# Half of a copy moved from ScalarE to VectorE, a store and a fill reordered on SyncE's queue, and an earlier bias add

## The chip, the cores and the metric

One core of a Trainium2 chip runs the whole kernel. The metric is the device time of one execution in microseconds; the time of a kernel is the median of its runs. TensorE (PE), VectorE (DVE), ScalarE (ACT), GpSimd (POOL) and SyncE (SP) each work through a program of their own in order, and wait for one another through semaphores. SyncE, ScalarE and GpSimd also issue the transfers (DMA).

## What is computed

One encoder layer on 512 tokens of 1024 features in fp32, then a final RMSNorm:

```
xn  = rmsnorm(h, g_mix)
proj = xn @ w_in + b_in                  # 1024 -> 2*512 (conv) + 3*512 (q, k, v)
conv = silu(layernorm(depthwise_conv31(a * sigmoid(g)) + conv_b))
attn = neighbourhood attention, 8 heads of 64, window 8 x 16, bias rpb[head, drow, dcol]
h   = h + [conv ; attn] @ w_out + b_out
h   = h + mixture of 32 experts, 4 of them for each token (clamped SwiGLU), on rmsnorm(h, g_ffn)
out = rmsnorm(h, g_final)
```

## The kernel before

Each fp32 product is made of three products: both operands are split into a high part (`..._high`, a cast made by ScalarE) and a low part (`..._low`, the difference, made by VectorE), and TensorE adds high x high, low x high and high x low.

**Start (to about 25 us).** The tokens are four tiles of 128. Per tile ScalarE squares and sums (L715), GpSimd makes rstd (L578, L580), VectorE makes xn (L1090), TensorE transposes it in two halves of four blocks into two PSUM banks (L1700), ScalarE copies each half to `xnT_high` (L703), and VectorE subtracts to get `xnT_low` (L1097). VectorE's program goes tile by tile: xn of tile n, then both low halves of tile n - 1. ScalarE's program puts the copies of tile 0 between the Squares of tile 2 and tile 3. Then VectorE copies the bias columns (L1102, L1103) and begins to split w_in (L1109).

**Projection (25 to about 141 us).** w_in comes in five loads of 2 MB (L467), issued by SyncE once x is loaded. TensorE makes 16 groups of 24 matmuls (L1714 to L1716; `proj_done` counts them), four for the gated input and its gate each, q and k, and then v by tiles. VectorE's program in the same time, written out by hand: the splits of w_in, the gated unit (L1117), 31 taps of the convolution for each of four channel blocks (L1130, L1134), and the bias tables of the eight heads (`tables`, L1154), two heads at a time, between splits and taps.

**Bias tables.** rpb is loaded to an SBUF tile (`rpb_tile`, 121 rows of 64 numbers) and stored 16 times to HBM (`rpb_pad`, L588, on GpSimd's queue). SyncE waits for all 16 stores (`rpb_stored`) and reads them back in another arrangement (`raw_bias`, L479), eight loads for each pair of heads. A pair's loads are issued only when the tables of the pair before are made, as they share a buffer.

**Zero fills.** The expert stage needs zeros in parts of `y_rows` in HBM. SyncE issues two fills from the SBUF tile `zeros` after the first pair's bias loads: the blocks past the thirtieth (`spare`, L482, counted by `y_stored`) and half-blocks of the others (L484). ScalarE waits for both before it copies v (L768, L769), as that overwrites `zeros`.

**b_out.** GpSimd adds it to h by four accumulating transfers (L593), once the eight tables are made. h is next used when w_out's products are added (L1197). After attention and w_out come the router and 32 experts with their weights streamed in; the change doesn't touch them.

Of the kernel before, what the change touches and what calls it, by code (L numbers as in the profile page):

```python
# [14 lines left out]
P = 128  # L15
SEQ, D_MODEL = 512, 1024
GRID_W, N_ROWS = 64, 8
QB = 16
NQ = GRID_W // QB
D_CONV, CONV_K = 512, 31  # L20
PAD = CONV_K // 2
HEADS, HEAD_DIM = 8, 64
# [13 lines left out]
CAP = 128  # L36
# [24 lines left out]
def encoder_kernel(nc, x, g_mix, w_in, b_in, conv_w, conv_b, ln_g, ln_b, rpb, w_out, b_out,  # L61
# [3 lines left out]
    with ctx:  # L65
        def sem(name):
            return ctx.enter_context(nc.semaphore(name))
# [70 lines left out]
        xnT_high = over("xnT_high", a_at, 0, [P, KD, SEQ])  # L138
# [35 lines left out]
        zeros = area_t[:, 2112:2112 + HALF]  # L174
# [126 lines left out]
        rstd_ready = sem("rstd_ready")  # L301
        xn_ready = sem("xn_ready")
        xn_transposed = sem("xn_transposed")
        xnT_first = sem("xnT_first")
        xnT_act = sem("xnT_act")
        xnT_low_ready = sem("xnT_low_ready")
        win_high_ready = sem("win_high_ready")
# [148 lines left out]
        @block.sync  # L456
        def _(sp):
            for n in range(NQ):
                sp.dma_start(h[:, n, :], x_blocks[n]).then_inc(x_loaded[n], 16)
            sp.dma_start(stage[0:20, 0, :], b_in[0].rearrange("(c p) -> c p", p=P)).then_inc(stage_loaded, 16)  # L460
            sp.dma_start(stage[0:CONV_K * CC, 1, :],
                         conv_w[0].rearrange("k (c p) -> (k c) p", p=P)).then_inc(stage_loaded, 16)

            for n in range(NQ):
                sp.wait_ge(x_loaded[n], 16)
            for i, col in enumerate((1, 0, 2, 3, 4)):
                sp.dma_start(unit(1 + i), win_v[:, :, col * HALF:(col + 1) * HALF]).then_inc(win_loaded[i], 16)  # L467

            spare = y_rows[LATE * CAP:, :].rearrange("(p i) (j f) -> p (i j) f", p=CAP, f=HALF)
            sp.wait_ge(rpb_stored, 16 * QB)  # L470
            copy_size = (HEADS * RPB_H + 1) * RPB_PITCH
            for pair in range(HEADS // 2):
                if pair:
                    sp.wait_ge(tables_ready, 8 * pair)
                for r in range(N_ROWS):
                    start = (2 * pair * RPB_H + WIN_H - 1 - r) * RPB_PITCH + QB - 1
                    src = bass.AP(rpb_pad.tensor, rpb_pad.offset + start,
                                  [[copy_size - 1, QB], [RPB_H * RPB_PITCH, 2], [1, RUN]])
                    sp.dma_start(raw_bias[r::N_ROWS, :, :], src).then_inc(raw_loaded, 16)  # L479
                if pair == 0:  # L480
                    sp.wait_ge(zeros_ready, 1)
                    sp.dma_start(spare, zeros[0:CAP].unsqueeze(1).to_broadcast([CAP, spare.shape[1], spare.shape[2]])).then_inc(y_stored, 16)  # L482
                    halves = y_rows[0:LATE * CAP, :].rearrange("(m s i) (j f) -> (i j) m s f", s=4, i=SMALL, f=HALF)[:, :, 2, :]
                    sp.dma_start(halves, zeros.unsqueeze(1).to_broadcast([P, LATE // 2, HALF])).then_inc(halves_zeroed, 16)  # L484
            def load(i, e):
                sp.dma_start(w_raw[i][:, :], piece_src(i, e)).then_inc(raw_piece[i], 16)

            sp.wait_ge(proj_done, 12)
            sp.dma_start(unit(1), wout_v[:, :, HALF:]).then_inc(wout_loaded[1], 16)
            sp.wait_ge(proj_done, 20)  # L490
            sp.dma_start(unit(6), wout_v[:, :, 0:HALF]).then_inc(wout_loaded[0], 16)
            for i in range(3):
                load(i, 0)
            sp.wait_ge(wout_done, 2 * NQ)
            for i in range(3, 5):
                load(i, 0)
            sp.wait_ge(xn2_stored, 16 * NQ)
            sp.wait_ge(xn2_transposed, 2 * NQ)
            sp.wait_ge(xg_loaded, 16)
            for i in (5, 6, 7, 8, 9, 11):  # L500
                load(i, 0)

            def reload(i, e, at):
                sp.wait_ge(piece_used, at + 1)
                load(i, e)

            def expert_at(b):
                return sp.value_load(order[0:1, bass.ds(b, 1)], min_val=0, max_val=N_EXPERTS - 1)

            sp.wait_ge(order_ready, 1)  # L510
            second = expert_at(1)
            for i in range(GATE, DOWN):
                if i == UP:
                    sp.wait_ge(overflow_ready, 2)
                    sp.wait_ge(gate_rows_ready, 1)
                    load(10, 0)
                reload(i, second, i)
            with sp.Fori(0, N_EXPERTS - 2) as j:
                e = expert_at(j + 2)
                for i in range(DOWN):  # L520
                    reload(i, e, PIECES * j + 8 + i)
                e = expert_at(j + 1)
                for i in range(DOWN, PIECES):
                    reload(i, e, PIECES * j + 8 + i)
            final = expert_at(N_EXPERTS - 1)
            for c in range(4):
                sp.wait_ge(piece_used, PIECES * (N_EXPERTS - 2) + 8 + UP + c + 1)
                sp.dma_start(w_raw[UP + c][:, :], piece_src(DOWN + c, final)).then_inc(raw_piece[UP + c], 16)
            trips = sp.value_load(n_ovf[0:1, 0:1], min_val=0, max_val=MAX_OVERFLOW)
            with sp.If(trips > 0):  # L530
                sp.wait_ge(late_added, NQ)
                with sp.Fori(0, trips) as t:
                    e = sp.value_load(ovf_exp[0:1, bass.ds(t, 1)], min_val=0, max_val=N_EXPERTS - 1)
                    for i in range(PIECES):
                        reload(i, e, EXTRA_BASE - PIECES + PIECES * t + i)
            for n in range(NQ):
                sp.wait_ge(final_ready, n + 1)
                sp.dma_start(out_blocks[n], out_tile[n]).then_inc(out_stored, 16)
            sp.wait_ge(out_stored, 16 * NQ)
# [3 lines left out]
        def _(pool):  # L543
# [39 lines left out]
                pool.wait_ge(ss_ready, n + 1)  # L583
                rstd_of(n, ss_ready)

            pool.wait_ge(rpb_tile_loaded, 16)
            for c in range(QB):
                pool.dma_start(rpb_pad[c], rpb_tile[:, :]).then_inc(rpb_stored, 16)  # L588

            pool.wait_ge(xn_ready, NQ)  # L590
            pool.wait_ge(tables_ready, 4 * HEADS)
            for n in range(NQ):
                pool.dma_start(h[:, n, :], row_bcast(b_out, D_MODEL), accum_op=ALU.add).then_inc(bout_added, 16)  # L593

# [97 lines left out]
        def _(act):  # L692
# [5 lines left out]
                              vec[0].rearrange("(c p) -> c p", p=P)).then_inc(stage_loaded, 16)  # L698
            def xnT_half(n):

                for half, high_done in enumerate((xnT_first, xnT_act)):
                    act.wait_ge(xn_transposed, 2 * n + half + 1)
                    s.copy(xnT_high[:, 4 * half:4 * half + 4, n * P:(n + 1) * P],  # L703
                           bank[4 + (2 * n + half) % 4][:, :].rearrange("p (k t) -> p k t", k=4)).then_inc(high_done, 1)

            def pT_out(i):

# [3 lines left out]
            for n in range(NQ):  # L711
                act.wait_ge(x_loaded[n], 16)
                if n:
                    act.wait_ge(ss_ready, n)
                s.activation(junk_norm[n % 2], h[:, n, :], ACT.Square, accum_out=ss[:, n:n + 1]).then_inc(ss_ready, 1)  # L715
                if n == NQ - 2:
                    xnT_half(0)
            for n in range(1, NQ):
                xnT_half(n)
            def win_high_part(g):  # L720
                loaded, high, _ = split_parts(g)
# [61 lines left out]

            act.wait_ge(glu_ready, 16)
            act.wait_ge(tables_ready, 1)
            act.wait_ge(y_stored, 16)
            act.wait_ge(halves_zeroed, 16)
            for n in range(NQ - 1):
                v_out(n)
# [265 lines left out]
        def _(dve):  # L1055
# [29 lines left out]
            for n in range(NQ + 1):  # L1085
                if n < NQ:
                    dve.wait_ge(rstd_ready, n + 1)
                    if n >= 2:
                        dve.wait_ge(xn_transposed, 2 * (n - 1))
                    v.scalar_tensor_tensor(xn_tile[:, n % 2, :], h[:, n, :], rstd[:, n:n + 1], gmix_row,  # L1090
                                           ALU.mult, ALU.mult).then_inc(xn_ready, 1)
                if n:
                    tokens = slice((n - 1) * P, n * P)
                    for half, high_done in enumerate((xnT_first, xnT_act)):
                        dve.wait_ge(high_done, n)
                        ks = slice(4 * half, 4 * half + 4)
                        v.tensor_tensor(xnT_low[:, ks, tokens],  # L1097
                                        bank[4 + (2 * (n - 1) + half) % 4][:, :].rearrange("p (k t) -> p k t", k=4),
                                        xnT_high[:, ks, tokens].bitcast(F32), ALU.subtract).then_inc(xnT_low_ready, 1)
# [45 lines left out]
            def tables(hd):  # L1145
                if hd == 0:
                    dve.wait_ge(mask_step, 15)
                    dve.wait_ge(proj_done, 8)
                dve.wait_ge(raw_loaded, 16 * N_ROWS * (hd // 2 + 1))

# [983 lines left out]
```

## Time and profile before

| | |
|---|---|
| median of 3 runs | 1336.9 us (1336.35 to 1338.11) |
| profiled execution | 1338.11 us, of it the span of the profile 1336.3 us |
| TensorE busy | 1269.6 us (95%) |
| VectorE busy | 1227.8 us (92%) |
| ScalarE, GpSimd busy | 972.3 us (73%), 182.7 us (14%) |
| moved by DMA | 473.31 MB, mean 354 GB/s |

The profile comes from one execution; times inside it are microseconds from the start of the span. SPq and ACTq are the queues of SyncE and ScalarE; the duration of an issue in them is how long the issuing program was held by it, and its landing is when the data was there. In a timeline the bracket behind a row gives the idle time before it and what ended it.

### The profile page before, as it was taken

The numbers are of one execution on the slowest core, as the hardware profiler recorded it, in microseconds if no ns is written. First come the engines' busy times: TensorE is split into PE (matmuls) and PEld (weight loads), VectorE is DVE, ScalarE is ACT, GpSimd is POOL, SyncE is SP. The second block draws the span as 40 slices with busy tenths as digits, with TensorE's granted clock in tenths as the row PEclk, the third lists the DMA queues.
The fourth block names the chain that finished last, engine by engine and source line by source line (L and its number), as shares of the span: only waits on it lengthen the run. The fifth ranks groups of instructions, "written<-read, shape, count | busy, mean of one in ns | idle before, by whom it ended". The sixth has DMA issues, their size and how long they took to land.

```text
span 1336.3 us, 17611 instructions
## 1 busy us (share of the span) xinstructions
PE 1269.6 (95%) x5771; PEld 1011.6 (76%) x5771; DVE 1227.8 (92%) x1010; ACT 972.3 (73%) x788; POOL 182.7 (14%) x181
## 2 busy tenths in 40 slices
PE   4999889789999999999999999999999999999996
PEld 4887668667878778787777777878777777777775
DVE  6799956699999999999999999999999999999997
ACT  4241664448797978788888888797979787878762
POOL 5001000112010101010110102020101010101252
PEclk9999889889999999999999999999999999999999
DMA  9945401499999999999999999999999999999984
GB/s 284 389 170 142 157 1 52 150 365 400 397 401 422 409 421 409 419 410 421 409 420 409 417 410 422 408 418 414 409 419 411 422 409 418 407 419 421 408 319 157
DMA packets 83974, 473.31 MB, mean 354 GB/s; under 512 B 10059, under 2 KB 10358, under 8 KB 34790
## 3 DMA queue, kind: packets, MB, share of 16 engines
q1 hardware_dynamic: 71726, 436.57, 81.1%
q0 software_dynamic: 7072, 19.39, 4.6%
q10 hardware_dynamic: 5144, 16.93, 3.4%
q8 instruction: 18, 0.29, 0.1%
q14 instruction: 14, 0.11, 0.0%
HBM read 447.72 MB, written 29.33 MB: 357 GB/s over the span
## 4 chain that ended last, share of the span: by engine, by line
PE 69%; DVE 15%; DMA 6%; ACT 5%; issue 3%; ACTq 1%; SPq 0%; POOL 0%; DVEq 0%
PE pair L1936 14%; PE pair L1937 13%; PE pair L1938 13%; PE pair L1952 6%; PE pair L1953 6%; DMA w_raw<-in_w_up 6%; DVE w_low L1283 5%; DVE area_m L1134 4%; ACT w_high L833 2%; PE pair L1923 2%; PE pair L1971 2%; PE pair L1950 1%; PE pair L1714 1%; PE pair L1715 1%; PE pair L1716 1%
## 5 line engine op out<-in xcount | busy, mean ns | idle before, releaser
L1283 DVE TENSOR_TENSOR w_low<-w_raw,w_high 128x2048 fp32r<-128x2048 f32 x380 | 838.2, 2245 | 41.3 <-ACT w_high L833 40.0
L833 ACT CAST w_high<-w_raw 128x2048 fp32r<-128x2048 f32 x380 | 703.0, 1878 | 170.5 <-PE pair L1938 117.5
L1936 PE MATMUL pair<-w_high,xT_high 128*128 128x512 f32 x528 | 211.2, 400 | 0.0
L1937 PE MATMUL pair<-w_low,xT_high 128*128 128x512 f32 x528 | 206.6, 391 | 0.0
L1938 PE MATMUL pair<-w_high,xT_low 128*128 128x512 f32 x528 | 206.0, 390 | 0.0
L1952 PE MATMUL pair<-w_high,xS 128*128 128x512 f32 x450 | 183.3, 407 | 0.1
L1953 PE MATMUL pair<-w_low,xS 128*128 128x512 f32 x450 | 175.7, 390 | 0.0
L1936 PEld LDWEIGHTS pair<-w_high,xT_high 128*128 128x128 f32 x528 | 99.1, 188 | 31.9 <-issue 11.4
L1938 PEld LDWEIGHTS pair<-w_high,xT_low 128*128 128x128 f32 x528 | 99.2, 188 | 21.6
L1937 PEld LDWEIGHTS pair<-w_low,xT_high 128*128 128x128 f32 x528 | 99.2, 188 | 19.2
L1936 PE MATMUL pair<-w_high,hT_high 128*128 128x512 f32 x256 | 102.1, 399 | 11.1 <-DVE w_low L1283 11.1
L1952 PEld LDWEIGHTS pair<-w_high,xS 128*128 128x128 f32 x450 | 84.5, 188 | 21.8 <-issue 3.6
L1937 PE MATMUL pair<-w_low,hT_high 128*128 128x512 f32 x256 | 100.5, 393 | 0.0
L1938 PE MATMUL pair<-w_high,hT_low 128*128 128x512 f32 x256 | 100.3, 392 | 0.0
L1953 PEld LDWEIGHTS pair<-w_low,xS 128*128 128x128 f32 x450 | 84.6, 188 | 20.4 <-issue 3.6
L1952 PE MATMUL pair<-w_high,hS 128*128 128x512 f32 x240 | 95.0, 396 | 0.0
L1953 PE MATMUL pair<-w_low,hS 128*128 128x512 f32 x240 | 93.5, 389 | 0.0
L1134 DVE SCALAR_TENSOR_TENSOR area_m<-area_u,convT,area_m 128x512 f32<-128x512 f32 x120 | 84.0, 755 | 0.4
L615 POOL CAST sel_in<-is_expert 128x128 fp32r (+1 forms) x17 | 42.6, 2504 | 272.0 <-PE pair L1953 246.9
L1936 PEld LDWEIGHTS pair<-w_high,hT_high 128*128 128x128 f32 x256 | 48.4, 189 | 23.7 <-DVE w_low L1283 12.2
L618 POOL CAST shift_sel<-is_expert 64x64 fp32r x15 | 14.1, 938 | 362.3 <-PE pair L1938 354.1
L1938 PEld LDWEIGHTS pair<-w_high,hT_low 128*128 128x128 f32 x256 | 48.5, 189 | 10.4
(355 smaller groups left out, 1800.5 us busy)
## 6 DMA issues: line engine op xcount, KB each, us to landing
w_raw<-in_w_gate SPq DMA_DIRECT2D x128, 1024.0 KB, 15.5
w_raw<-in_w_up SPq DMA_DIRECT2D x128, 1024.0 KB, 16.9
w_raw<-in_w_down SPq DMA_DIRECT2D x128, 1024.0 KB, 16.8
ring<-in_w_in SPq DMA_DIRECT2D x5, 2048.0 KB, 18.7
y_rows<-area_t SPq DMA_DIRECT2D x1, 8704.0 KB
y_rows<-area_m ACTq DMA_DIRECT2D x15, 512.0 KB
ring<-in_w_out SPq DMA_DIRECT2D x2, 2048.0 KB, 7.9
y_rows<-area_t SPq DMA_DIRECT2D x1, 3840.0 KB, 38.6
```

The costliest lines, as they stand in the source:

```text
L615: g.tensor_copy(sel_in[:, :], is_expert[:, bass.ds(e, 1)].to_broadcast([P, CAP])).then_inc(sel_in_ready, 1)
L618: g.tensor_copy(shift_sel[SMALL:, SMALL:], is_expert[SMALL:, bass.ds(e, 1)].to_broadcast([SMALL, SMALL])).then_inc(sel_in_ready, 1)
L833: s.copy(w_high[:, i % HIGH_RING, raw:], w_raw[i][:, raw:]).then_inc(high_ready, 1)
L1134: v.scalar_tensor_tensor(mixedT[:, c, :], u_pad[:, c, k:k + SEQ], convT[:, k * CC + c:k * CC + c + 1], mixedT[:, c, :], ALU.mult, ALU.add) ...
L1283: v.tensor_tensor(w_low[i][:, raw:], w_raw[i][:, raw:], w_high[:, i % HIGH_RING, raw:].bitcast(F32), ALU.subtract).then_inc(low_ready, 1)
L1923: last = t.transpose(bank[6 + k // 4][:, (k % 4) * CAP:(k % 4 + 1) * CAP], h_tok[:, k::KD], ident[0:CAP, 0:CAP])
L1936: t.matmul(to[half], tok_high, hi, start=(opens and kk == 0), stop=False)
L1937: t.matmul(to[half], tok_high, lo, start=False, stop=False)
L1938: last = t.matmul(to[half], tok_low, hi, start=False, stop=(k == KD - 1))
L1952: t.matmul(to[half], rows, w_high[:, i % HIGH_RING, cols], start=(opens and kk == 0), stop=False)
L1953: last = t.matmul(to[half], rows, w_low[i][:, cols], start=False, stop=(k == KD - 1))
L1971: t.matmul(to[half], sel[:, :], rows[:, half * HALF:(half + 1) * HALF], start=True, stop=False)
```

## The change

Four edits, all ahead of the expert stage:

1. ScalarE copies only the second half of each transposed tile, and does so after all four Squares. VectorE copies the first half itself, right ahead of the two subtractions.
2. The `spare` fill is issued by SyncE right behind the loads of w_in. The 16 stores of rpb_pad move from GpSimd's queue to SyncE's, behind this fill. The half-block fill stays behind the first pair's bias loads.
3. The wait for the `spare` fill moves from ScalarE (ahead of the v copies) to VectorE (ahead of the first bias table).
4. GpSimd issues the b_out transfers after twelve projection groups, and not after the tables.

```diff
@@ SyncE
             spare = y_rows[LATE * CAP:, :].rearrange("(p i) (j f) -> p (i j) f", p=CAP, f=HALF)
+            sp.wait_ge(zeros_ready, 1)
+            sp.dma_start(spare, zeros[0:CAP].unsqueeze(1).to_broadcast([CAP, spare.shape[1], spare.shape[2]])).then_inc(y_stored, 16)
+            sp.wait_ge(rpb_tile_loaded, 16)
+            for c in range(QB):
+                sp.dma_start(rpb_pad[c], rpb_tile[:, :]).then_inc(rpb_stored, 16)
             sp.wait_ge(rpb_stored, 16 * QB)
...
                 if pair == 0:
-                    sp.wait_ge(zeros_ready, 1)
-                    sp.dma_start(spare, zeros[0:CAP].unsqueeze(1).to_broadcast([CAP, spare.shape[1], spare.shape[2]])).then_inc(y_stored, 16)
@@ GpSimd
-            pool.wait_ge(rpb_tile_loaded, 16)
-            for c in range(QB):
-                pool.dma_start(rpb_pad[c], rpb_tile[:, :]).then_inc(rpb_stored, 16)
-
             pool.wait_ge(xn_ready, NQ)
-            pool.wait_ge(tables_ready, 4 * HEADS)
+            pool.wait_ge(proj_done, 12)
@@ ScalarE
-                for half, high_done in enumerate((xnT_first, xnT_act)):
-                    act.wait_ge(xn_transposed, 2 * n + half + 1)
-                    s.copy(xnT_high[:, 4 * half:4 * half + 4, n * P:(n + 1) * P],
-                           bank[4 + (2 * n + half) % 4][:, :].rearrange("p (k t) -> p k t", k=4)).then_inc(high_done, 1)
+                act.wait_ge(xn_transposed, 2 * n + 2)
+                s.copy(xnT_high[:, 4:8, n * P:(n + 1) * P],
+                       bank[4 + (2 * n + 1) % 4][:, :].rearrange("p (k t) -> p k t", k=4)).then_inc(xnT_act, 1)
...
-                if n == NQ - 2:
-                    xnT_half(0)
-            for n in range(1, NQ):
+            for n in range(NQ):
                 xnT_half(n)
...
-            act.wait_ge(y_stored, 16)
@@ VectorE
                 if n:
+                    dve.wait_ge(xn_transposed, 2 * (n - 1) + 1)
                     tokens = slice((n - 1) * P, n * P)
-                    for half, high_done in enumerate((xnT_first, xnT_act)):
+                    v.tensor_copy(xnT_high[:, 0:4, tokens],
+                                  bank[4 + 2 * (n - 1) % 4][:, :].rearrange("p (k t) -> p k t", k=4)).then_inc(xnT_dve, 1)
+                    for half, high_done in enumerate((xnT_dve, xnT_act)):
                         dve.wait_ge(high_done, n)
...
             def tables(hd):
                 if hd == 0:
                     dve.wait_ge(mask_step, 15)
+                    dve.wait_ge(y_stored, 16)
                     dve.wait_ge(proj_done, 8)
```

## Rows read from the trace of the kernel before

**Rows 1.** The page, part 4: shares of the chain that ended last.
```profile
PE 69%; DVE 15%; DMA 6%; ACT 5%; issue 3%; ACTq 1%; SPq 0%; POOL 0%; DVEq 0%
```

**Rows 2.** The chain of waits, 0 to 330 us: start, us, what.
```profile
24.86 0.77 PE pair L1714
...
71.56 1.23 DVE area_u L1117 x4
```

**Rows 3.** Busy time by stretch.
```profile
core 0: us, PE busy (x) PEld busy (x) DVE busy (x) ACT busy (x) POOL busy (x), PEclk, DMA share, GB/s
...
44.00:47.00 3.00, 3.00 (x15) 2.49 (x14) 2.86 (x5) 1.63 (x2) 0.00 (x0) 1.00 1.08 274
...
50.00:70.00 20.00, 20.00 (x89) 16.54 (x89) 19.39 (x32) 3.24 (x4) 0.00 (x0) 1.00 1.05 408
...
78.00:80.00 2.00, 2.00 (x11) 1.65 (x10) 2.00 (x4) 1.58 (x2) 0.00 (x0) 1.00 0.15 57
```

**Rows 4.** Timeline of ScalarE, 0 to 62 us.
```profile
14.67 1.06 ACT L715 ACTIVATE area_t<-h 128x1024 f32<-128x1024 f32 x1
...
28.68 2.94 ACT L730 CAST glu_high<-ring 128x1024 fp32r<-128x1024 f32 x3 [5.32 <-DMA ring<-in_w_in]
```

**Rows 5.** Timeline of VectorE, 0 to 62 us.
```profile
15.41 1.27 DVE L1090 SCALAR_TENSOR_TENSOR area_q<-h,rstd,area_k 128x1024 f32<-128x1024 f32 x1
```

**Rows 6.** Timeline of SyncE's queue, from several stretches up to 106 us.
```profile
14.41 16.26 SPq L467 DMA_DIRECT2D ring<-in_w_in  x5
...
25.48 5.18 SPq L467 DMA_DIRECT2D ring<-in_w_in  x1
...
30.71 5.55 SPq L479 DMA_DIRECT2D area_m<-rpb_pad  x1
...
40.73 0.59 SPq L479 DMA_DIRECT2D area_m<-rpb_pad  x1
...
42.03 20.55 SPq L484 DMA_DIRECT2D y_rows<-area_t  x1
78.95 26.72 SPq L479 DMA_DIRECT2D area_m<-rpb_pad  x24
...
100.69 1.80 SPq L479 DMA_DIRECT2D area_m<-rpb_pad  x3
```

**Rows 7.** Groups of VectorE's instructions by form, 0 to 300 us.
```profile
L1270 DVE COPY area_q<-pair 128x512 f32<-128x512 f32 x2 | 1.4, 685 | 0.0
```

**Rows 8.** Timeline of GpSimd, 0 to 62 and 90 to 260 us.
```profile
17.32 8.47 POOL L588 DMA_DIRECT2D rpb_pad<-area_t  x16
...
111.90 3.64 POOL L593 DMA_DIRECT2D h<-in_b_out  x4 [86.11 <-DVE ring L1154]
```

**Rows 9.** Timeline of VectorE, 60 to 165 us.
```profile
75.51 0.68 DVE L1154 SCALAR_TENSOR_TENSOR area_t<-area_m 128x192 f32<-128x192 f32 x2
...
86.39 0.68 DVE L1154 SCALAR_TENSOR_TENSOR area_t<-area_m 128x192 f32<-128x192 f32 x2
...
107.93 0.68 DVE L1154 SCALAR_TENSOR_TENSOR area_t<-area_m 128x192 f32<-128x192 f32 x2
```

**Rows 10.** DMA issues, 0 to 300 us; last column median to landing.
```profile
y_rows<-area_t SPq DMA_DIRECT2D x1, 3840.0 KB, 38.6
area_m<-rpb_pad SPq DMA_DIRECT2D x32, 64.0 KB, 2.3
h<-in_b_out POOLq DMA_DIRECT2D x4, 512.0 KB, 8.6
...
rpb_pad<-area_t POOLq DMA_DIRECT2D x16, 30.2 KB, 4.8
```

**Rows 11.** DMA issues, 41 to 42 us, the bias load issued last.
```profile
area_m<-rpb_pad SPq DMA_DIRECT2D x1, 64.0 KB, 8.6
```

**Rows 12.** DMA issues, 26 to 31 us, the w_in load issued last.
```profile
ring<-in_w_in SPq DMA_DIRECT2D x1, 2048.0 KB, 22.5
```

**Rows 13.** Timeline of ScalarE, 92 to 96 us.
```profile
93.32 0.69 ACT L748 ACTIVATE area_q<-pair,small 128x512 f32<-128x512 f32 x1 [3.81 <-PE pair L1716]
```

**Rows 14.** Busy time by stretch, columns as in the third group.
```profile
152.00:172.00 20.00, 17.28 (x90) 13.32 (x88) 16.62 (x41) 11.83 (x35) 0.00 (x0) 0.66 0.15 59
192.00:196.00 4.00, 3.93 (x22) 3.68 (x21) 1.63 (x9) 2.18 (x9) 0.00 (x0) 0.65 0.00 0
```

More of the change, by code:

```diff
@@ L303, in encoder_kernel @@
         xn_transposed = sem("xn_transposed")
-        xnT_first = sem("xnT_first")
+        xnT_dve = sem("xnT_dve")
         xnT_act = sem("xnT_act")
```

## The prediction

> **What bounds the kernel now.** I read the page first: of the chain that ended last PE has 69% and VectorE 15% [rows 1]. The diff touches only what runs before the expert loop, so the chain of waits of the first 330 us came next, and it shows who sets the pace there [rows 2]. TensorE begins the projection with w_in at 24.86, and the chain stays on its matmuls until 71.56. There it goes over to VectorE, and it stays on VectorE's program (splits of w_in, bias tables, convolution taps) without an idle gap to about 135. Attention and the router follow on the same chain. So every microsecond by which 24.86 moves, or by which VectorE stalls between 71 and 135, should arrive at the end. Nothing in that stretch waits for a fixed time: the weights of the expert loop are fetched on counts of finished projections.
>
> Then the timelines (VectorE and ScalarE at the start, SyncE's queue, VectorE at the tables) and the table of stretches. Transfers are the hidden resource: between 50 and 70 the DMA engines are full at 408 GB/s [rows 3], and what flows there is the zero fill of y_rows, which nobody needs before 120. The reader should see how near the small transfers lie to their use: each group of eight bias loads comes in just ahead of the table that reads it.
>
> **Part 1, half of the xnT_high copies goes from ScalarE to VectorE.** Before, ScalarE puts the two copies of tile 0 ahead of the Square of tile 3 (which starts at 14.67 [rows 4]), and VectorE goes to xn of tile 2 at 15.41 [rows 5]. After, ScalarE squares all four tiles first. The Square of tile 3 cannot start before its x is there, about 14.4 (SyncE waits for the same load and sends w_in at 14.41 [rows 6]); with the 1.1 us of a Square (1.06 busy) the one copy left for tile 0 runs at 15.5 and ends at 16.05 (0.58 busy). VectorE, which works in order, waits for it ahead of xn of tile 2, and subtracts for 0.6: xn of tile 2 starts at 16.7 and not 15.41.
>
> From there VectorE has two xn (1.27 busy, of which the next operation overlaps some 0.08: 1.2 each), and for each of the tiles 1, 2 and 3 one copy and two subtractions, nine operations. The same kind of copy stands in the router stage, 0.69 us busy like a subtraction [rows 7], 0.6 when the next follows at once. So 16.7 + 2.4 + 9 x 0.6 = 24.5 where before it was 23.0 (after them come 0.5 us of column copies and the first split of w_in, 1.2, and then the matmul of 24.86). The idle time inside the old sequence is already used up in this. ScalarE's part ends about 24.4, in time for the split. Four hand-overs inside VectorE may add up to 0.3. I take 1.6 us; ends 1.3 (no hand-over costs anything, x comes a little earlier) and 2.2 (a tenth more for each of the six operations that follow a hand-over). The cover: none. TensorE waits for exactly this split before 24.86, and its second group's weights come for either start in time (ScalarE starts on them at 28.68 [rows 4], and the first group's 24 matmuls last until 33.3), so the whole 1.6 reaches 71.56. Nothing else is late.
>
> **Part 2, the order on SyncE's queue.** Before, GpSimd issues the 16 stores of rpb_pad at 17.32 (8.47 us [rows 8]) and SyncE, when the five w_in issues end (14.41 + 16.26 = 30.7), sends eight bias loads, then the big fill, then the half-block fill [rows 6]. After, the order on SyncE is w_in, big fill (8704 KB), 16 stores, wait for all of them, eight loads, half-block fill (3840 KB). What is late is the first table, at 75.51 [rows 9]. Step by step:
> - From 44 to 47 the rate falls to 274 GB/s, from about 390 to 408 on either side: that is the passage of the eight small loads, so w_in's bytes are through at 44 and the fills begin at 47; 12.85 MB at 0.408 MB/us are 31.5 us, which ends at 78.5 as the table of stretches shows [rows 3]. After, w_in is rid of the stores' 0.5 MB (1.2 us), so the big fill runs from 42.8 for 21.8 us to 64.6.
> - An issue behind the fill doesn't return at once: the half-block fill's issue took 20.55 us, until 62.58, 15.6 us after the big fill began to flow [rows 6]. The first store's issue should return 15.6 after 42.8, at 58.4. Fifteen more at 0.6 (issues of this queue when nothing blocks it: three in 1.80 from 100.69, so the eighth starts some 4.4 after the first [rows 6]) end at 67.4; landing takes 2.3 (bias loads) to 4.8 (the old stores beside w_in) [rows 10]: 69.7 to 72.2.
> - Eight loads, 4.4 + 2.3 = 6.7: the first pair of tables has its data at 76.5 to 79. One engine or two trickle at 57 GB/s for 2.3 us behind a fill [rows 3], a reason against the low end. I take 77.6.
> - VectorE wants the table at 75.51 + 1.6 = 77.1. Parts 1 and 2 don't add, the later of the two counts: 77.6 - 75.51 = 2.1 us. The new wait for the big fill, ahead of the same table, ends long before (about 67), and behind it stand all of VectorE's splits and taps, for which TensorE waits in turn.
>
> **Part 2, second pair.** Its loads are asked for when the first tables are made (3.44 us after the first starts) and are needed 7.44 us after that (78.95 to 86.39 [rows 6, 9]), and take 6.8: they have 0.65 to spare. The half-block fill used to be nearly over by then (issued at 42.03, landed 38.6 later [rows 6, 10]). After, it is issued at 69.8 + 4.95 = 74.8, flows from 76 for 9.6 us and has its tail to 87.9. The loads sit behind it. Before, the last of the eight behind w_in landed 1.3 us after it (40.73 + 8.6 = 49.3 [rows 6, 11] against 25.48 + 22.5 = 48.0 [rows 12]); so 89.2, with the need at 77.6 + 3.44 + 7.44 = 88.5. I take 0.7, ends 0 and 3.
>
> **Part 3, b_out at twelve projections.** It starts at 93.32 + the delay (when ScalarE takes up the twelfth) instead of 111.90 [rows 8, 13]. Its four issues take 3.6 us and each transfer 8.6 [rows 10], together some 13, so they run while the third and fourth pair of loads come in; those have 0.7 and 0.5 us to spare (the latter: last issue at 105.1, landed 107.4, table at 107.93 [rows 9]). A load that shares engines should need up to twice its 2.3; but most of b_out is over at 106. I take 0.5, ends 0 and 2.5. Its old place cost nothing and it saves nothing: h is next touched past 200.
>
> **A rule that speaks against part 2.** The rows: stores on GpSimd's queue landed in 4.8 us although w_in filled the engines, while a bias load, on SyncE's own queue behind w_in, took 8.6 where alone it takes 2.3 [rows 10, 11]. The Trainium skill (DMA: Bandwidth & Descriptors, Queues, rings and completion order) says that an engine takes turns between queue rows by packet, but takes one ring's descriptors in order. By that rule the stores lose their turns and stand behind the whole fill, as I reckoned from the rows; without it they would be in HBM near 51 (the issue next after w_in returned at 36.3 [rows 6], sixteen at 0.6, and 4.8 to land) and part 2 would cost nothing; that is the first rival below. The old landing times agree with the rule; no row of before shows a small store behind a fill.
>
> The ScalarE wait for the big fill that goes cost nothing: it was reached after 120. Sum: 2.1 + 0.7 + 0.5 = 3.3 us. On the profiled execution (1338.1, span 1336.3) that gives 1341.4; it lay 1.2 above the median of the runs, so **1340.2 us**.
>
> **Rivals.**
> - Only the start counts (1.6 us or less): the fill lets the stores pass, or drains sooner, and the tables find their data. For it: 76.5 is a possible arrival, and I place the stall by differences of half a microsecond between long transfers. Against it: the 20.55 us issue. Time 1336.9 + 1.6 = 1338.5, with the start at its low end 1338.2.
> - The queue costs more: 121 rows of 256 bytes to a store may drain slowly, tables reached at 80 (4.5), the second pair 3, b_out 2.5: 10 us, 1346.9.
> - Faster, by the clock. At 152 to 172 the granted clock is 0.66 with TensorE busy 17.28 of the 20 us, and 0.65 at 192 to 196 with 3.93 [rows 14]. Full clock would save 0.34 x 17.28 + 0.35 x 3.93 = 7.3 us at most. If the shift leaves TensorE without these low stretches, 1336.9 + 3.3 - 7.3 = 1332.9. The sign turns once more than 3.3 of the 7.3 is saved, the 0.2% once more than 6. Against it: everything moves together, so the sparse pattern ahead of the drop comes again; and much of this busy time is beside other work. The same could go the other way.
> - The change does nothing (everything is covered): no; VectorE had no cover for its copies.
>
> **How the numbers follow.** 0.2% is 2.7 us, about what a measurement of this kernel can tell from no change. Forecast (2.7 to 7 us more) 0.50, costly queue 0.09, start only 0.33, faster clock 0.08 (of which 0.02 stays within the bound). Slower 0.59, same 0.34, faster 0.07. The forecast's own range is 1339.6 to 1344. The range for 8 in 10 takes in the start-only case with some gain of clock, 1336.5, and most of the costly queue, 1345.
>
> **What the new profile would show.** First matmul of the projection near 26.4, xn of tile 2 at 16.7. On SyncE's queue the first store's issue as a long one, until about 58, the last store near 67. A gap of VectorE ahead of the first table, ended by a DMA, first table at 77 to 79. A smaller gap ahead of the third table. b_out near 96. From 135 on the same steps as before, 3 us later. The prediction is wrong if the first store's issue returns at once, if VectorE goes without a gap from 73 to 135, if the ring behaves otherwise with small rows, or if TensorE's clock falls at other places.

## The result

The change makes the kernel slower: 1346.64 us against 1338.11 us for the kernel before, timed beside it (medians of seven runs each), a ratio of 1.0057 with a 95% interval of 1.0040 to 1.0075, so 7.6 us (5.4 to 10.0); the two medians alone lie 8.5 us apart. I had forecast 3.3 us more. The direction was right, the size was not. The median of the kernel before is 1.2 us higher here than the one that the prediction started from, so the difference, and not the absolute time, is what to compare. The granted clock adds scatter: three of the seven runs, at a mean granted clock of 0.977, took 1348.5 to 1349.3 us, the four at 0.980 to 0.983 took 1343.4 to 1346.6.

### The profile after

This is one execution of 1343.44 us with a span of 1341.7 us (the seven runs lie between 1343.4 and 1349.3; it is one of the shorter ones). The page's head and its chain (answer to [rows 1]):

```profile
span 1341.7 us, 17612 instructions
...
PE 67%; DVE 14%; DMA 7%; ACT 6%; issue 3%; SPq 1%; ACTq 1%; POOL 0%; DVEq 0%
```

TensorE and VectorE have lost shares to DMA, ScalarE and SyncE's queue. The timeline of VectorE at the start (answers to [rows 5]):

```profile
15.72 0.69 DVE L1098 TENSOR_TENSOR xnT_low<-pair,xnT_high 128x512 fp32r<-128x512 f32 x1 [0.71 <-ACT xnT_high L704]
16.33 1.28 DVE L1088 SCALAR_TENSOR_TENSOR area_q<-h,rstd,area_k 128x1024 f32<-128x1024 f32 x1
```

VectorE waits 0.71 us for ScalarE's one copy of tile 0 and starts xn of tile 2 at 16.33. TensorE's timeline (answers to [rows 2]):

```profile
26.34 0.76 PE L1716 MATMUL pair<-xnT_high,glu_high 128*128 128x512 f32 x1 [3.59 <-DVE win_low L1110]
```

The first matmul starts at 26.34 where it was 24.86. But x came 0.44 us earlier in this execution (ScalarE's first Square starts at 7.58, before at 8.02), so by these two traces the edit itself cost 1.9. SyncE's queue (answers to [rows 6]; the last row is the first store's issue by itself):

```profile
14.13 15.22 SPq L467 DMA_DIRECT2D ring<-in_w_in  x5
29.39 5.30 SPq L471 DMA_DIRECT2D y_rows<-area_t  x1
34.73 33.26 SPq L477 DMA_DIRECT2D rpb_pad<-area_t  x16
69.11 5.03 SPq L487 DMA_DIRECT2D area_m<-rpb_pad  x8
74.18 0.59 SPq L490 DMA_DIRECT2D y_rows<-area_t  x1
79.55 33.33 SPq L487 DMA_DIRECT2D area_m<-rpb_pad  x24
...
34.73 22.77 SPq L477 DMA_DIRECT2D rpb_pad<-area_t  x1
```

The first store's issue alone is held for 22.77 us, until 57.5. The 16 are issued by 68.0, and the first bias load goes at 69.11. The tables on VectorE (answers to [rows 9]):

```profile
76.14 0.67 DVE L1156 SCALAR_TENSOR_TENSOR area_t<-area_m 128x192 f32<-128x192 f32 x2
...
89.02 0.69 DVE L1156 SCALAR_TENSOR_TENSOR area_t<-area_m 128x192 f32<-128x192 f32 x2 [1.93 <-DMA area_m<-rpb_pad]
...
104.59 0.68 DVE L1156 SCALAR_TENSOR_TENSOR area_t<-area_m 128x192 f32<-128x192 f32 x2 [4.61 <-DMA area_m<-rpb_pad]
...
115.14 0.66 DVE L1156 SCALAR_TENSOR_TENSOR area_t<-area_m 128x192 f32<-128x192 f32 x2
```

The four pairs of tables start 0.6, 2.6, 7.3 and 7.2 us later than before. So there is no gap ahead of the first pair, 1.93 us ahead of the second, and 4.61 us ahead of the third. The chain of waits shows what the second and the third waited for (start, us, what):

```profile
80.12 1.37 SPq L487
...
86.58 2.42 DMA area_m<-rpb_pad
...
96.94 7.62 DMA area_m<-rpb_pad
```

The second pair's loads stood behind the half-block fill. The second to the fourth were slow to be issued, 1.37 us each instead of 0.6, and the first, issued at 79.55, landed 7.4 us later at 86.98, just behind the fill itself (issued at 74.18, landed at 86.69). Two short stretches of the DMA issues have both:

```profile
y_rows<-area_t SPq DMA_DIRECT2D x1, 3840.0 KB, 12.5
...
area_m<-rpb_pad SPq DMA_DIRECT2D x1, 64.0 KB, 7.4
```

The last load of the third pair was issued in time and then took 7.62 us to land instead of 2.3. What ran beside it stands in GpSimd's timeline (answers to [rows 8, 10]):

```profile
94.52 3.69 POOL L595 DMA_DIRECT2D h<-in_b_out  x4 [78.40 <-PE pair L1718]
```

and in the list of DMA issues:

```profile
h<-in_b_out POOLq DMA_DIRECT2D x4, 512.0 KB, 10.9
```

b_out's four transfers start 2 us after the third pair's first load; the median of their landings is 10.9 us after the issue.

### The profile page after: what moved, and what is told of

It is laid out like the page before. It is cut to its first block, busy times and chain, and to the rows that moved or that the text cites. A ratio compares the mean times of both kernels' runs of the same rounds, so it can differ in the third digit from the quotient of the medians.

```text
span 1341.7 us, 17612 instructions
## 1 busy us (share of the span) xinstructions
PE 1270.3 (95%) x5771; PEld 1012.1 (75%) x5771; DVE 1230.4 (92%) x1014; ACT 969.7 (72%) x784; POOL 174.0 (13%) x165
## 4 chain that ended last, share of the span: by engine, by line
PE 67%; DVE 14%; DMA 7%; ACT 6%; issue 3%; SPq 1%; ACTq 1%; POOL 0%; DVEq 0%
PE pair L1938 14%; PE pair L1939 13%; PE pair L1940 13%; DMA w_raw<-in_w_up 6%; PE pair L1954 5%; PE pair L1955 5%; DVE w_low L1285 5%; ACT w_high L831 3%; DVE area_m L1135 3%; PE pair L1925 2%; PE pair L1973 2%; PE pair L1952 1%; PE pair L1716 1%; PE pair L1717 1%; PE pair L1718 1%
## 5 line engine op out<-in xcount | busy, mean ns | idle before, releaser
L1938 PE MATMUL pair<-w_high,hT_high 128*128 128x512 f32 x256 | 102.0, 399 | 10.9 <-DVE w_low L1285 10.9
L620 POOL CAST shift_sel<-is_expert 64x64 fp32r x15 | 14.6, 971 | 363.1 <-PE pair L1940 363.1
## 6 DMA issues: line engine op xcount, KB each, us to landing
w_raw<-in_w_up SPq DMA_DIRECT2D x128, 1024.0 KB, 16.7
```

The source lines that it names most:

```text
L620: g.tensor_copy(shift_sel[SMALL:, SMALL:], is_expert[SMALL:, bass.ds(e, 1)].to_broadcast([SMALL, SMALL])).then_inc(sel_in_ready, 1)
L1938: t.matmul(to[half], tok_high, hi, start=(opens and kk == 0), stop=False)
```

## The experiments

Each kernel was timed with the kernel before beside it in five rounds. The medians of before were 1336.7, 1337.7 and 1336.6 us in the three sets. "gaps" are idle times of VectorE ended by a bias load, ahead of the four pairs of tables.

### First set: the parts alone

**b_out early, all else as before.**

```diff
-            pool.wait_ge(tables_ready, 4 * HEADS)
+            pool.wait_ge(proj_done, 12)
```

> The kernel before with the b_out edit alone (wait for twelve projections). Theory A (overlap): b_out costs what its packets take from the bias loads in flight beside them, one packet of 0.29 us ahead of each of theirs. Here the third pair's loads start at 89.8 and are all but home when b_out's data flows at 95, and the fourth pair's (100.7 to 105.6) meet its second half. Gap ahead of the third table 0 to 1 us, ahead of the fourth 0.5 to 2, time 1 to 3 us longer. Theory B (fixed price): b_out costs the 4.6 us of the changed kernel wherever it starts among the pairs; 4.5 to 5 us longer.

Ratio 1.0033 (1.0020 to 1.0046), 4.4 us longer. VectorE's timeline:

```profile
99.13 0.68 DVE L1154 SCALAR_TENSOR_TENSOR area_t<-area_m 128x192 f32<-128x192 f32 x2 [3.41 <-DMA area_m<-rpb_pad]
```

The whole price sits ahead of the third pair, nothing ahead of the fourth. By time it is nearer to theory B, though the gap, 3.41 us, is smaller than B's 4.6. Theory A had the place wrong: I thought the third pair's loads would be all but home. Seven were. The DMA issues of two short stretches, with the seventh load (issued at 91.93) and then the eighth (issued at 92.56):

```profile
area_m<-rpb_pad SPq DMA_DIRECT2D x1, 64.0 KB, 2.9
...
area_m<-rpb_pad SPq DMA_DIRECT2D x1, 64.0 KB, 6.5
```

The eighth took 6.5 us and landed at 99.10, where the table was waiting. One load of 64 KB, met by b_out's first data, holds VectorE for 3.4 us. The packets of the DMA engines show how. Between 94.6 and 96.4, with the eighth load under way, they are (packets, MB, share of 16 engines; q0 is GpSimd's queue; SyncE's, q1, has no line, as it has no packet here):

```profile
q0 software_dynamic: 83, 0.34, 101.8%
```

For 1.8 us not one packet of the bias load started.

**The change with b_out put back.**

```diff
-            pool.wait_ge(proj_done, 12)
+            pool.wait_ge(tables_ready, 4 * HEADS)
```

> The changed kernel with b_out back behind all tables. Theory A and B: the 4.6 us gap ahead of the third table goes, the 1.9 us gap ahead of the second stays; taps end 2.6 us later than before, time 2.6 us longer than before. Rival (the rest of the difference lies elsewhere, for instance in TensorE's granted clock in the attention stage): still 5 us or more longer.

Ratio 1.0043 (1.0029 to 1.0057), 5.7 us longer. The 4.61 us gap is gone, the one ahead of the second pair is 1.51. The tables come some 3 us late with the start, the measured time says 5.7; it was run again (third set).

**The copies alone** (ScalarE's and VectorE's part of the change, and no other).

> The kernel before with the copy edit alone. Theory (as the two traces show it): the first projection matmul starts 1.5 us later but fewer of its matmuls run at the slow rate, so that VectorE's gated unit starts only 0.6 us later; time 0.6 us longer, not told from none. My prediction's step: the whole 1.6 us arrives.

Ratio 1.0012 (1.0004 to 1.0021), 1.6 us longer, with no gaps. The prediction's step held and not the reading of two traces: how many of the first group's 24 matmuls take 0.43 us instead of 0.227 differs from execution to execution, 14 in the trace of before, 10 in that of after, 6 to 13 in the experiments (none in the one made to remove them), at either start. The first tables of the two traces lie only 0.6 us apart because of this chance and of the earlier x.

**The order on SyncE's queue alone** (fill and stores ahead of the bias loads on SyncE, wait for the fill on VectorE).

```diff
+            sp.wait_ge(zeros_ready, 1)
+            sp.dma_start(spare, ...).then_inc(y_stored, 16)
+            sp.wait_ge(rpb_tile_loaded, 16)
+            for c in range(QB):
+                sp.dma_start(rpb_pad[c], rpb_tile[:, :]).then_inc(rpb_stored, 16)
             sp.wait_ge(rpb_stored, 16 * QB)
...
                     dve.wait_ge(mask_step, 15)
+                    dve.wait_ge(y_stored, 16)
```

> The kernel before with the fill and stores on SyncE's queue in the new order, with its wait, alone. Theory: no gap ahead of the first table or 0.3 us (the first pair lands about 76), a gap of 2 to 2.6 us ahead of the second pair's, no gap ahead of the third and fourth; time 2 to 2.6 us longer. Rival (prediction's split): most of the cost sits ahead of the first table.

Ratio 1.0024 (1.0013 to 1.0035), 3.2 us longer. VectorE's timeline:

```profile
75.57 0.68 DVE L1153 SCALAR_TENSOR_TENSOR area_t<-area_m 128x192 f32<-128x192 f32 x2 [1.26 <-DMA area_m<-rpb_pad]
...
88.97 0.68 DVE L1153 SCALAR_TENSOR_TENSOR area_t<-area_m 128x192 f32<-128x192 f32 x2 [2.42 <-DMA area_m<-rpb_pad]
```

With the earlier start VectorE asks for the first pair at 74.3 and its data comes at 75.5. So the first pair's data is late too, and in the full change the copy edit hides that, as I had said: the later of the two counts, not their sum.

### Second set: what in each part costs

**b_out written and not added** (this leaves x out of the residual; the experts' loads become uneven, so that its total time of 1509.57 us can't be compared, and only the first 110 us are read).

```diff
-                pool.dma_start(h[:, n, :], row_bcast(b_out, D_MODEL), accum_op=ALU.add).then_inc(bout_added, 16)
+                pool.dma_start(h[:, n, :], row_bcast(b_out, D_MODEL)).then_inc(bout_added, 16)
```

> As the b_out edit alone, but the four transfers write b_out over h and don't add it (this leaves out x in the residual). Theory A (it is the adding: each engine has a 3.7 KB add packet of 0.29 us in turn with every packet of the bias loads, and there is 2 MB to read as well as to write): plain packets are about half as long, b_out is gone in half the time, the gap ahead of the third table falls from 3.4 to 0 to 1.5 us and the time to 0 to 2 us above before. Theory C (any transfer on another queue takes the same turns): the gap stays near 3.4 and the time near 4.4 above.

b_out lands in 6.4 us instead of 9.7, but the gap grows:

```profile
100.34 0.68 DVE L1154 SCALAR_TENSOR_TENSOR area_t<-area_m 128x192 f32<-128x192 f32 x2 [4.55 <-DMA area_m<-rpb_pad]
```

The last two loads took 6.6 and 6.7 us, no less than beside the adding transfers. The adding is not what costs; theory A is out. Of the larger gap 1.1 us is that the eighth load was issued later (93.66, in the edit alone 92.56). Here too no packet of SyncE's queue started for 1.8 us (94.4 to 96.2):

```profile
q0 software_dynamic: 171, 0.63, 102.2%
```

**Only the big fill first, the stores on GpSimd's queue as before.**

```diff
+            sp.wait_ge(zeros_ready, 1)
+            sp.dma_start(spare, ...).then_inc(y_stored, 16)
             sp.wait_ge(rpb_stored, 16 * QB)
...
-                    sp.dma_start(spare, ...).then_inc(y_stored, 16)
```

> The kernel before with only the big fill moved ahead of the first bias loads on SyncE's queue; the stores stay on GpSimd's. Theory (the stores behind the fill are what delays the first and so the second pair): the first pair's loads sit behind the fill and land near 68, ahead of the need at 74 to 75.5, the half-block fill goes as before; no gaps, time within 1 us of before. Rival (the fill's order itself does it): gaps as in the order edit, 3 us longer.

Ratio 0.9998 (0.9989 to 1.0007), and no gaps. SyncE's queue:

```profile
30.44 6.09 SPq L471 DMA_DIRECT2D y_rows<-area_t  x1
36.58 29.88 SPq L481 DMA_DIRECT2D area_m<-rpb_pad  x8
66.50 1.60 SPq L484 DMA_DIRECT2D y_rows<-area_t  x1
77.48 26.79 SPq L481 DMA_DIRECT2D area_m<-rpb_pad  x24
```

The first pair's loads wait behind the fill, but it is one passage. With the stores on this queue there are two, one after the other, since the loads read what the stores wrote: the stores are issued until 68.0 in the full change, and the loads only then.

**The order edit with the half-block fill behind the last pair's loads.**

```diff
                     sp.dma_start(raw_bias[r::N_ROWS, :, :], src).then_inc(raw_loaded, 16)
-                if pair == 0:
-                    halves = ...
-                    sp.dma_start(halves, ...).then_inc(halves_zeroed, 16)
+            halves = ...
+            sp.dma_start(halves, ...).then_inc(halves_zeroed, 16)
```

> The order edit alone, with the half-block fill moved behind the fourth pair's loads. Theory: the gap ahead of the second pair's table (2.4 us in the order edit alone) goes, the 1.3 us gap ahead of the first stays; time 1 to 1.5 us above before instead of 3.2. Rival (the second pair is late because the first is late): the gap stays, time 3 us above.

Ratio 1.0016 (1.0006 to 1.0026), 2.1 us longer where the order edit alone cost 3.2. VectorE's timeline:

```profile
76.29 0.67 DVE L1152 SCALAR_TENSOR_TENSOR area_t<-area_m 128x192 f32<-128x192 f32 x2 [0.87 <-DMA area_m<-rpb_pad]
87.19 0.67 DVE L1152 SCALAR_TENSOR_TENSOR area_t<-area_m 128x192 f32<-128x192 f32 x2
```

The gap ahead of the second pair is gone, the one ahead of the first stays. So the second gap is the half-block fill. The times by themselves would not tell the two kernels apart (0.8 to 3.5 and 1.7 to 4.7 us), the gaps do.

**TensorE kept busy ahead of its first group.**

```diff
+            for _ in range(12):
+                t.transpose(bank[1][:, 0:P], ident[:, :], ident[:, :])
             pe.wait_ge(xnT_low_ready, 2 * NQ)
```

> The kernel before with twelve transposes of the identity into an unused bank, run by TensorE while it waits for the first split of w_in. In the runs so far 7 to 14 of the first group's 24 matmuls went at the slow rate (0.43 against 0.227 us). Theory (the idle 3 to 4 us ahead of the first matmul are why it starts slow): 0 to 5 slow ones, VectorE's gated unit 1 to 2.5 us earlier, time 1 to 2 us below before. Rival: slow matmuls stay 7 to 14 whatever precedes them, time the same.

No slow matmul is left (TensorE's timeline):

```profile
21.51 2.73 PE L1710 MATMUL pair<-ident 128*128 128x128 f32 x12
25.07 0.47 PE L1716 MATMUL pair<-xnT_high,glu_high 128*128 128x512 f32 x1 [0.83 <-DVE win_low L1109]
```

Ratio 0.9991 (0.9979 to 1.0003), 1.2 us less, not told from none. Of all versions it points furthest below the kernel before. In five traces whose record of the granted clock reaches back far enough (the b_out edit alone is one) the slow matmuls are those run at the lower of the two clock levels, 0.50 or 1.2 GHz, which TensorE had been given while it sat idle; the stretches of that trace (columns as in [rows 3]):

```profile
24.00:26.00 2.00, 1.58 (x4) 1.32 (x5) 0.28 (x1) 0.00 (x0) 1.17 (x3) 0.50 1.06 398
...
28.00:30.00 2.00, 2.00 (x10) 1.68 (x9) 0.56 (x1) 1.64 (x2) 0.00 (x0) 0.99 1.05 402
```

### Third set: how b_out holds a small load, and whether a stall arrives

**b_out in quarters of 256 columns, 16 transfers.**

```diff
-                pool.dma_start(h[:, n, :], row_bcast(b_out, D_MODEL), accum_op=ALU.add).then_inc(bout_added, 16)
+                for q in range(4):
+                    cols = slice(q * 256, (q + 1) * 256)
+                    pool.dma_start(h[:, n, cols], row_bcast(b_out, 256, q * 256), accum_op=ALU.add).then_inc(bout_added, 16)
```

> As the b_out edit alone, but each of its four transfers is sent as four of 256 columns (16 in all). In the b_out edit alone a bias load issued at 92.56 took 6.5 us to land where one just before b_out's data took 2.9. Theory D (a bias load waits for whole packets of the other queue, and a packet holds several rows of a transfer): packets a quarter as long, loads beside b_out land in 3 to 4 us, the gap ahead of the third table falls from 3.4 to 0 to 1.5 us. Theory E (it is the share of the engines' time that counts, however it is cut): loads take 6 us again, gap near 3.4, b_out over at the same time or later.

Ratio 1.0035 (1.0022 to 1.0048), 4.7 us longer. VectorE's timeline:

```profile
97.82 0.68 DVE L1156 SCALAR_TENSOR_TENSOR area_t<-area_m 128x192 f32<-128x192 f32 x2 [1.64 <-DMA area_m<-rpb_pad]
...
110.42 0.68 DVE L1156 SCALAR_TENSOR_TENSOR area_t<-area_m 128x192 f32<-128x192 f32 x2 [1.86 <-DMA area_m<-rpb_pad]
```

The gap ahead of the third pair is halved, and the last loads take 4.4 and 3.7 us. Between 94.6 and 96.4 SyncE's packets now get through beside GpSimd's:

```profile
q0 software_dynamic: 209, 0.19, 74.1%
q1 hardware_dynamic: 54, 0.08, 15.6%
```

That speaks for theory D; the engines are also less full here (74% for b_out). But 16 issues hold GpSimd for 14.6 us, b_out now reaches into the fourth pair, and the rest of the gap turns up there.

**A stall without a transfer.**

```diff
             def tables(hd):
+                if hd == 4:
+                    v.tensor_reduce(bank[7][:, 0:1], xnT_high[:, :, :]..., AX.X, ALU.add)
```

> The kernel before with one reduction of 4096 columns on VectorE ahead of the third pair's tables, whose result nobody reads: a stall of 4.2 to 4.5 us in the place of b_out's gap and no transfer moved. Theory (VectorE's stall reaches the end in full and nothing else is added): 4.2 to 4.5 us longer. Rival (a stall there also costs granted clock in the attention stage): 6 us or more longer. Rival (part is made good later): 2 us or less.

VectorE's timeline:

```profile
96.55 4.42 DVE L1147 TENSOR_REDUCE pair<-xnT_high 128x1 f32<-128x4096 f32 x1
```

4.42 us on VectorE's timeline give a ratio of 1.0043 (1.0026 to 1.0059), 5.7 us (3.5 to 7.9). So a stall at this place arrives, at least 3.5 of its 4.4 us; the rival by which it is made good later (2 us or less) is out, the one by which it costs some clock besides (6 us or more) is not.

**One b_out transfer early, three late.**

```diff
-            pool.wait_ge(tables_ready, 4 * HEADS)
+            pool.wait_ge(proj_done, 12)
             for n in range(NQ):
+                if n == 1:
+                    pool.wait_ge(tables_ready, 4 * HEADS)
```

> As the b_out edit alone, but only the first tile's transfer goes after twelve projections, the other three after all tables. Theory D and E: the last bias load of the third pair meets one transfer of 2.7 us instead of four; its landing 2.9 to 5 us instead of 6.5, gap ahead of the third table 0 to 2 us, time 0 to 2 us above before. Rival F (any transfer started there costs its own fixed latency): gap 3.4 as with four.

VectorE's timeline:

```profile
98.06 0.68 DVE L1156 SCALAR_TENSOR_TENSOR area_t<-area_m 128x192 f32<-128x192 f32 x2 [2.32 <-DMA area_m<-rpb_pad]
```

The last load (issued at 92.60) takes 5.4 us, the gap is 2.32 us, two thirds of that of four transfers: more than D and E gave. Its ratio of 1.0033 (1.0020 to 1.0046) is above what the gap explains. The table of stretches (columns as in [rows 3]) shows when this one transfer ended:

```profile
96.00:97.00 1.00, 1.00 (x7) 0.81 (x6) 0.00 (x0) 0.21 (x1) 0.00 (x0) 1.00 1.01 203
97.00:98.00 1.00, 1.00 (x6) 0.84 (x5) 0.00 (x0) 0.69 (x1) 0.00 (x0) 1.00 0.29 80
98.00:99.00 1.00, 1.00 (x6) 0.83 (x5) 0.94 (x3) 0.00 (x0) 0.00 (x0) 1.00 0.00 0
```

The load landed at 98.04, the transfer beside it at 98.10: when that one was through, and not by its own size.

**The change with b_out put back, again.**

> The changed kernel with b_out back behind all tables, a second time, because its first time (5.7 us above before) was 2.5 more than the parts add up to (copies 1.6, gap ahead of the second pair 1.5). Theory (that was chance in the clock of the attention stage): 3 to 4 us above before. Rival (the two parts together cost more than each): 5 to 6 us again.

Ratio 1.0035 (1.0020 to 1.0050), 4.7 us. Between the two expectations; the two sets together give some 5.2. The parts (1.6 for the copies, 3.2 for the order) sum to 4.8, less the first gap that is not paid twice. What is above that goes with the granted clock (a split made after the times were seen). Of this run's eleven executions seven at a mean of 0.982 or more took 1337.7 to 1341.4 us (median 1339.5, 2.9 above before), and four at 0.977 or 0.978 took 1344.8 to 1347.0. The profiled one is among the four; two stretches of it:

```profile
160.00:180.00 20.00, 17.80 (x93) 13.44 (x93) 12.80 (x34) 11.63 (x32) 0.00 (x0) 0.72 0.00 0
180.00:200.00 20.00, 16.45 (x82) 12.23 (x82) 11.16 (x33) 10.57 (x37) 0.00 (x0) 0.70 0.01 2
```

The copies alone had 0.77 and 0.91 there. The first time three of six executions had 0.978. So the surplus is mostly such executions, as the theory said; why they come more often here than in the kernel before is open.

## Why the prediction was right and wrong

**Part 1, the copies: right.** xn of tile 2 was put at 16.7 and started at 16.33 with an x that came 0.44 earlier; the first matmul was put at 26.4 and came at 26.34, which with the x of before would have been 26.8, so this agreement is partly luck. The cost, 1.6 us, was measured as 1.6 us (0.5 to 2.8).

**Part 2, the queue ahead of the first pair: right in its steps.** First store's issue back at 58.4, measured 57.5; last store issued at 67.4, measured 68.0; the data a little late for a kernel with the early start (gap 1.26 us in the order edit alone) and hidden by the copies' delay in the full change, where the gap that I forecast ahead of the first table did not appear. I had put the data at 77.6; it was there at 75.8. What made it late is that stores and loads depend on each other and each had to pass this queue, as the run with the fill alone shows (no cost). The rule of the Trainium skill (DMA: Bandwidth & Descriptors, Queues, rings and completion order), that an engine takes one ring's descriptors in order, agrees with the landings: with the fill alone moved, the first bias load was issued at 36.6 and landed at 66.6, 30 us later.

**Part 2, the second pair: right, with two errors that cancel.** I put the last load's landing at 89.2, and the table began at 89.02, 2.6 us later than before where the two steps of part 2 summed to 2.8. The gap was larger than my 0.7 (1.93, and 2.42 in the order edit alone) because VectorE was ready at 87.1 and not at 88.5: the first tables had not been held until 77.6 but had begun at 76.14. (For the fill I had let the first pair's loads start at 69.8, for the first pair's data at 70.9; it was 69.11.) The slow issues of 1.37 us I had not foreseen; no run separates how much of the 1.93 us is theirs.

**Part 3, b_out: this step failed.** The prediction said: "A load that shares engines should need up to twice its 2.3; but most of b_out is over at 106. I take 0.5, ends 0 and 2.5." The gap was 4.61 us, and the edit alone cost 4.4 us (2.7 to 6.1). Two things were wrong in it. I took a small load to pay a share of its own duration, when it pays for what it finds ahead of it: 6.5 instead of 2.3 us for a single load in the edit alone, 7.6 for the last of four in the full change. And I gave the third pair 0.7 us to spare, when in the trace of before it had 0.12: its last load is issued only at 94.91, since the issue ahead of it took longer, and lands 2.2 us later, for a table at 97.27. The row for it, from the DMA issues of before at 95.0 to 95.4:

```profile
area_m<-rpb_pad SPq DMA_DIRECT2D x1, 64.0 KB, 2.2
```

Even twice its 2.3 us, less the 0.7, would have made 1.6 us and not 0.5. In the full change the queue edit had besides pushed this pair's loads (first one at 92.44, before 89.83) right under b_out (94.52), so that the last four and not the last one were held. So the edits meet: each is priced with the other's timing. The whole miss lies here: up to the second pair the trace is 2.6 us late with 2.8 forecast, at the third it is 7.3 with 3.3 forecast.

What holds the load is shown in part. It is not the adding (plain transfers: gap 4.55 us). The load does not get a thinner share, it gets nothing for 1.8 us at a time, and it goes with the size of the pieces on the other queue (quarters: 4.4 us for a load in place of 6.5, and packets of both queues in the same stretch; one transfer: it lands when that one is through). By estimate from the packets of the edit alone (83 in 1.8 us on 16 engines, 0.35 us each, eight of 4 KB to an engine in a transfer of 512 KB), one transfer keeps an engine for some 2.8 us. That fits the same section of the Trainium skill, by which an engine drains a whole packet from one queue row before it turns to another; no run shows the packets' bounds, and why the faster plain transfers held the load no less stays open.

**The sum.** 1.6 for the copies, 1.93 and 4.61 for the gaps make 8.1 us; measured 7.6 (5.4 to 10.0). The run with a bare stall shows that such a gap reaches the end, at least for the most part. The total stands on the gaps of one trace and the parts' timings agree with it (1.6 + 3.2 + 4.4 = 9.2, with an overlap of the first gap and the copies); but the change with and without b_out differ by only some 2.4 us (7.6 against 5.2). In the traces, where both start alike (first matmul 26.34 and 26.34), b_out puts the fourth table 4.4 us later (115.14 against 110.76); the difference of the times carries the executions at a low granted clock, so it is known no better than to 2 us.

**The rivals.** "The queue costs more" came close to the time (1346.9 us, measured 1346.64) by luck: its 10 us lie at the edge of the interval, they start from a median 1.2 us lower, and most of them were in the wrong part. The 256-byte rows drained without trouble, the first bias load went 1.1 us behind the last store's issue, and the first tables were reached at 76.14 and not 80. "Only the start counts" is out by the gaps. "Faster by the clock" did not come: between 140 and 220 the granted clock was 1.00, 0.74, 0.95 and 0.97 by stretches of 20 us, before 0.85, 0.81, 0.91 and 1.00. But its size is real as scatter: the same kernel with b_out put back took 1337.7 to 1347.0 us, by its clock.

## What to carry to other kernels

A transfer that "costs nothing" where it is may stand there because small transfers just ahead of their use share its engines: before you move a bulk transfer, list the small ones that will then be in flight, with what the last of each group has to spare. A small load beside bulk on another queue pays for the bulk ahead of it and not twice its own time; and a store and a load that depends on it should not both pass a queue behind a fill. Price edits of one change together, since one moves the traffic under the other.

## What the runs showed of the hardware

- An issue on SyncE's queue behind a fill of 8.9 MB holds SyncE's program for 20.6 us before and 22.8 after, and even a short one behind a fill of 3.9 MB takes 1.4 us instead of 0.6.
- A 64 KB load took 2.3 us alone and 6.5 beside 512 KB transfers of GpSimd's queue, added or plain, and 4.4 beside 128 KB ones. Beside the 512 KB transfers no packet of the load started for 1.8 us; beside the 128 KB ones 54 packets of its queue did in the same stretch.
- After 3 to 4 us of idle time TensorE ran 6 to 14 of its first 24 matmuls at 0.43 us instead of 0.227, at a granted clock of 0.50 where the record shows it, a different number in each execution, which alone moves what follows by up to 1.6 us; with transposes in the idle time none. Two traces that are compared to half a microsecond should be aligned for that first.
- Executions of one kernel differ by several us, and the time goes with TensorE's mean granted clock: 1337.7 to 1341.4 us at 0.982 or more, 1344.8 to 1347.0 at 0.978 or less, in one set of eleven.
